# Second block's two modulated norms: latent and context parts signalled apart, all latent chunks first at the second norm, three preparing operations moved

## Reference

```
for layer in range(2):
    u  = rms_norm_2(h,  norm_g[layer]) * (1 + scale)   + shift
    uc = rms_norm_2(hc, norm_g[layer]) * (1 + scale_c) + shift_c
    layer 0: y, yc = ab_mixer(u, uc, ...)     # in projections of u and uc, two attentions
    layer 1: y, _  = c_mixer(u, uc, ...)      # q, k, v, z = split(u @ in_w); q_c, k_c, v_c, z_c of uc
    h = h + gate * y;   hc = hc + gate_c * yc # context only in layer 0
return rms_norm_2(h, final_g)
```

## Time and profile before

| | us |
|---|---|
| median of three runs | 2233.18 |
| the profiled execution | 2232.56 |
| its span | 2230.2 |
| PE busy | 2177.5 |
| DVE busy | 1262.2 |
| ACT busy | 903.3 |

### The profile page before, as it was taken

How to read it: one execution, slowest core, us unless ns; L and a number is a source line. 1 busy time by engine, 2 the same in 40 slices (tenths; PEclk the granted TensorE clock), 3 DMA queues, 4 the chain that set the end, 5 groups by cost and what they waited for, 6 DMA issues and landing times.

```text
span 2230.2 us, 31483 instructions
## 1 busy us (share of the span) xinstructions
PE 2177.5 (98%) x12755; PEld 1784.1 (80%) x12755; DVE 1262.2 (57%) x1752; ACT 903.3 (41%) x1575; POOL 289.0 (13%) x215
## 2 busy tenths in 40 slices
PE   7999999999999999999999999999999999999998
PEld 6776688778888776688778888989888887888777
DVE  4687548984224687548983226422666636212794
ACT  4447843222214447843222223232565524212673
POOL 2001322121222001322121000000010000000230
PEclk9999999999999999999999999999999999999999
DMA  5220016543563220025543322132000122321221
GB/s 164 90 71 2 1 61 204 183 145 80 149 171 91 90 71 1 1 67 198 189 146 79 135 95 60 48 101 72 15 23 9 52 76 94 123 68 57 72 72 57
DMA packets 149106, 194.26 MB, mean 87 GB/s; under 512 B 43165, under 2 KB 96426, under 8 KB 148962
## 3 DMA queue, kind: packets, MB, share of 16 engines
q1 hardware_dynamic: 110288, 169.83, 23.4%
q10 hardware_dynamic: 38514, 22.26, 3.8%
q0 software_dynamic: 160, 0.16, 0.0%
HBM read 180.51 MB, written 11.72 MB: 86 GB/s over the span
## 4 chain that ended last, share of the span: by engine, by line
PE 89%; DVE 5%; ACT 3%; issue 2%; DMA 0%; ACTq 0%; POOLq 0%; DVEq 0%
PE ps L536 69%; PE ps L2779 3%; PE ps L1903 3%; PE ps L2796 2%; PE ps L2808 2%; PE ps L2317 1%; PE ps L2274 1%; PE ps L2303 1%; DVE probs_t L2118 1%; PE ps L2784 1%; PE ps L1937 1%; ACT probs_t L2885 1%; DVE neg_max L2085 1%; PE ps L2782 1%; PE ps L744 1%
## 5 line engine op out<-in xcount | busy, mean ns | idle before, releaser
L501 DVE TENSOR_TENSOR w_low<-w_raw,w_high 128x2048 fp32r<-128x2048 f32 (+4 forms) x140 | 303.1, 2165 | 493.1 <-ACT w_high L496 493.0
L496 ACT ACTIVATE w_high<-w_raw 128x2048 fp32r<-128x2048 f32 (+4 forms) x140 | 253.2, 1808 | 574.0 <-PE ps L536 550.6
L536 PE MATMUL ps<-h_hi,w_high 128*128 128x512 f32 (+1 forms) x1168 | 439.7, 376 | 3.0 <-DVE w_low L501 2.2
L536 PE MATMUL ps<-h_lo,w_high 128*128 128x512 f32 (+1 forms) x1168 | 437.1, 374 | 0.0
L536 PE MATMUL ps<-h_hi,w_low 128*128 128x512 f32 (+1 forms) x1168 | 436.8, 374 | 0.0
L536 PEld LDWEIGHTS ps<-h_hi,w_high 128*128 128x128 f32 x1168 | 219.9, 188 | 53.9 <-issue 10.5
L536 PEld LDWEIGHTS ps<-h_hi,w_low 128*128 128x128 f32 x1168 | 219.8, 188 | 39.8
L536 PEld LDWEIGHTS ps<-h_lo,w_high 128*128 128x128 f32 x1168 | 220.0, 188 | 39.0 <-issue 0.5
L536 PE MATMUL ps<-w_high,h_hi 128*128 128x512 f32 (+3 forms) x576 | 215.0, 373 | 0.7 <-DVE h_lo L3181 0.7
L536 PE MATMUL ps<-w_low,h_hi 128*128 128x512 f32 (+3 forms) x576 | 212.1, 368 | 0.0
L536 PE MATMUL ps<-w_high,h_lo 128*128 128x512 f32 (+3 forms) x576 | 211.8, 368 | 0.0
(11 more groups left out here) (395 smaller groups left out, 3674.3 us busy)
## 6 DMA issues: line engine op xcount, KB each, us to landing
w_raw<-in_w_gate_up SPq DMA_DIRECT2D x44, 1024.0 KB, 5.1
ada_w<-in_ada_w SPq DMA_DIRECT2D x24, 1024.0 KB, 5.2
w_raw<-in_w_down SPq DMA_DIRECT2D x20, 1024.0 KB, 5.0
w_raw<-in_w_in SPq DMA_DIRECT2D x16, 1024.0 KB, 5.1
w_raw<-in_c_in_w SPq DMA_DIRECT2D x16, 1024.0 KB, 5.8
w_raw<-in_w_out SPq DMA_DIRECT2D x8, 1024.0 KB, 4.8
w_raw<-in_ab_in_w SPq DMA_DIRECT2D x8, 1024.0 KB, 5.2
masked_scratch<-mask_table ACTq DMA_DIRECT2D x8, 512.0 KB, 3.6
```

The costliest lines, as they stand in the source:

```text
L496: e.activation(w_high[j % 2][:, 0:size], w_raw[j % 2][:, 0:size], ACT.Copy).then_inc(sig.w_high_done, 1)
L501: e.tensor_tensor(w_low[j % 2][:, 0:size], w_raw[j % 2][:, 0:size], w_high[j % 2][:, 0:size].bitcast(F32), ALU.subtract).then_inc(sig.w_lo ...
L536: mm = e.matmul(dst, lhs, rhs, start=start and a == 0, stop=stop and a == 2)
```

## The change

`full_ready`, `part_high` and `part_low` now count latent parts alone, and `ctx_full`, `ctx_high` and `ctx_low` count the context's. At the first norm (`l == 0`) the parts alternate, latent and context of chunk 0, of chunk 1 and so on, and `full` runs one part ahead of `low`. At the second norm all eight latent chunks come first, `full` and `low` of a chunk right behind each other, then the eight context parts, paired. `ModGain`'s operations move from ahead of the reciprocal to behind the second staging copy of the first norm. The product behind the first norm waits for a context chunk at tile 4; the product that first reads the context of layer 1 waits for all of it once. The load of `gate_first` also waits for the second norm's transposes, which are long done when it is issued.

```diff
+                            if self.context_paced and i == 0 and n == NT:
+                                e.wait_ge(sig.ctx_low, B["ctx_low"] - self.paced + k + 1)
+                            if self.context_whole and i == 0 and n == 0 and k == 0:
+                                e.wait_ge(sig.ctx_low, B["ctx_low"])
...
+                self.l, self.sum_bank, self.wide_banks, self.context, self.gains = l, sum_bank, wide_banks, context, gains
+                self.full, self.high, self.low = (sig.full_ready, sig.ctx_full), (sig.part_high, sig.ctx_high), (sig.part_low, sig.ctx_low)
+                self.full_name, self.high_name, self.low_name = ("full_ready", "ctx_full"), ("part_high", "ctx_high"), ("part_low", "ctx_low")
+                self.parts = [(k, v) for k in range(KD) for v in range(2)] if l == 0 else [(k, v) for v in range(2) for k in range(KD)]
...
-                for k in range(KD):
-                    e.wait_ge(sig.full_ready, B["full_ready"] + k + 1)
-                    for src, nt, t0, v in self.halves:
-                        ins = e.activation(h2_hi[:, k, t0:t0 + nt], mod_full[:, k % 2, t0:t0 + nt], ACT.Identity, bias=self.shift(k, v))
-                    ins.then_inc(sig.part_high, 1)
-                    if k == 4:
+                for k, v in self.parts:
+                    _, nt, t0, _ = self.halves[v]
+                    e.wait_ge(self.full[v], B[self.full_name[v]] + k + 1)
+                    e.activation(h2_hi[:, k, t0:t0 + nt], mod_full[:, k % 2, t0:t0 + nt], ACT.Identity, bias=self.shift(k, v)).then_inc(self.high[v], 1)
+                    if (k, v) == (4, 1 - self.l):
...
+                if self.gains:
+                    self.gains.make(e, B, ch)
+                    e.wait_ge(sig.mod_ready, B["mod_ready"] + 1)
...
+                def full(k, v):
+                    src, nt, t0, _ = self.halves[v]
                     if k >= 2:
-                        e.wait_ge(sig.part_low, B["part_low"] + k - 1)
...
+                        e.wait_ge(self.low[v], B[self.low_name[v]] + k - 1)
...
-                def low(k):
-                    e.wait_ge(sig.part_high, B["part_high"] + k + 1)
-                    for src, nt, t0, v in self.halves:
-                        ins = e.scalar_tensor_tensor(out=h2_lo[:, k, t0:t0 + nt], in0=mod_full[:, k % 2, t0:t0 + nt], scalar=self.shift(k, v),
-                                                     in1=h2_hi[:, k, t0:t0 + nt].bitcast(F32), op0=ALU.add, op1=ALU.subtract)
-                    ins.then_inc(sig.part_low, 1)
-                    if k == 4:
+                    if k == 0:
+                        e.wait_ge(sig.inverse_wide, B["inverse_wide"] + v + 1)
+                    dst, x, inv = mod_full[:, k % 2, t0:t0 + nt], src[:, k, :], ps[:, self.wide_banks[v], 0:nt]
+                    if self.l and v == 0:
+                        cuts = [(by_blocks(dst)[:, :, j], by_rows(x)[:, :, j], by_rows(inv)[:, :, j]) for j in range(4)]
+                    else:
+                        cuts = [(dst, x, inv)]
+                    for dst, x, inv in cuts:
+                        ins = e.scalar_tensor_tensor(out=dst, in0=x, scalar=self.gain(k, v), in1=inv, op0=ALU.mult, op1=ALU.mult)
+                    ins.then_inc(self.full[v], 1)
+
+                def low(k, v):
+                    _, nt, t0, _ = self.halves[v]
+                    e.wait_ge(self.high[v], B[self.high_name[v]] + k + 1)
+                    e.scalar_tensor_tensor(out=h2_lo[:, k, t0:t0 + nt], in0=mod_full[:, k % 2, t0:t0 + nt], scalar=self.shift(k, v),
+                                           in1=h2_hi[:, k, t0:t0 + nt].bitcast(F32), op0=ALU.add, op1=ALU.subtract).then_inc(self.low[v], 1)
+                    if (k, v) == (4, 1 - self.l):
                         cut_low(e, B, 1, 2048)
...
-                full(0)
-                low(0)
-                full(1)
-                for k in range(1, KD):
-                    if k + 1 < KD:
-                        full(k + 1)
-                    low(k)
+                if self.l:
+                    for k, v in self.parts[:KD]:
+                        full(k, v)
+                        low(k, v)
+                    paired = self.parts[KD:]
+                else:
+                    paired = self.parts
+                full(*paired[0])
+                for now, after in zip(paired, paired[1:]):
+                    full(*after)
+                    low(*now)
+                low(*paired[-1])
...
+            def make(self, e, B, ch):
                 e.wait_ge(sig.mod_landed, B["mod_landed"])
...
+                e.wait_ge(sig.inverse_wide, B["inverse_wide"])
...
-        mod_norms = [ModNorm(0, 6, (7, 0), context), ModNorm(1, 0, (1, 2))]
+        mod_norms = [ModNorm(0, 6, (7, 0), context, ModGain()), ModNorm(1, 0, (1, 2))]
...
-            context, ModGain(),
+            context,
...
+                b.context_paced = a.l == 0
...
+            if isinstance(b, PairAhead):
+                a.context_whole = True
```

More of the change, by code:

```diff
@@ L383, in build_program @@
         sig.full_ready = semaphore("full_ready")
+        sig.ctx_full = semaphore("ctx_full")
+        sig.ctx_high = semaphore("ctx_high")
+        sig.ctx_low = semaphore("ctx_low")
         sig.part_high = semaphore("part_high")
@@ L548, in build_program @@
             paced = 0
+            context_paced = context_whole = False
             chase = False
@@ L3079, in build_program, with __init__ @@
             chase = True
-            late = ("part_high", "part_low", "full_ready", "sq_ready", "sq_added")
-            def __init__(self, l, sum_bank, wide_banks, context=None):
-                self.l, self.sum_bank, self.wide_banks, self.context = l, sum_bank, wide_banks, context
+            late = ("part_high", "part_low", "full_ready", "ctx_high", "ctx_low", "ctx_full", "sq_ready", "sq_added")
+            def __init__(self, l, sum_bank, wide_banks, context=None, gains=None):
+                self.l, self.sum_bank, self.wide_banks, self.context, self.gains = l, sum_bank, wide_banks, context, gains
+                self.full, self.high, self.low = (sig.full_ready, sig.ctx_full), (sig.part_high, sig.ctx_high), (sig.part_low, sig.ctx_low)
+                self.full_name, self.high_name, self.low_name = ("full_ready", "ctx_full"), ("part_high", "ctx_high"), ("part_low", "ctx_low")
+                self.parts = [(k, v) for k in range(KD) for v in range(2)] if l == 0 else [(k, v) for v in range(2) for k in range(KD)]
                 self.halves = [(x_t, S, 0, 0), (xc_t, CTX, S, 1)]
@@ L3087, in __init__ @@
                 self.counts = {"sq_ready": self.nv * KD, "sq_added": self.nv * (KD - 1), "sum_step": 1, "root_ready": 1, "inv_ready": 1,
-                               "staged_ready": 2, "inverse_wide": 2, "full_ready": KD, "part_high": KD, "part_low": KD}
+                               "staged_ready": 2, "inverse_wide": 2, "full_ready": KD, "part_high": KD, "part_low": KD,
+                               "ctx_full": KD, "ctx_high": KD, "ctx_low": KD}
+                if gains:
+                    self.counts.update(gains.counts)
             def gain(self, k, v):
@@ L3151, in tensor @@
                     mm.then_inc(sig.inverse_wide, 1)
-                    release(bank, B, ("full_ready", KD))
+                    release(bank, B, (self.full_name[v], KD))
             def vector(self, e, B, L, ch):
@@ L3159, in vector @@
                     e.tensor_copy(mod_stage[:, a:b, :], bc(mod_inv[:, a:b].unsqueeze(2), [P, b - a, P])).then_inc(sig.staged_ready, 1)
-                def full(k):
+                if self.gains:
[3 more added lines that the diff above has]
+                    src, nt, t0, _ = self.halves[v]
                     if k >= 2:
-                        e.wait_ge(sig.part_low, B["part_low"] + k - 1)
-                    if k == 4 and self.context:
+                        e.wait_ge(self.low[v], B[self.low_name[v]] + k - 1)
+                    if (k, v) == (4, 1) and self.context:
@@ L3176, in full @@
-                    ins.then_inc(sig.full_ready, 1)
-                def low(k):
-                    e.wait_ge(sig.part_high, B["part_high"] + k + 1)
-                    for src, nt, t0, v in self.halves:
-                        ins = e.scalar_tensor_tensor(out=h2_lo[:, k, t0:t0 + nt], in0=mod_full[:, k % 2, t0:t0 + nt], scalar=self.shift(k, v),
-                                                     in1=h2_hi[:, k, t0:t0 + nt].bitcast(F32), op0=ALU.add, op1=ALU.subtract)
-                    ins.then_inc(sig.part_low, 1)
-                    if k == 4:
-                        cut_low(e, B, 1, 2048)
```

7 lines of the change are left out of this document (2 added, 5 removed).

## The result

The changed kernel takes 2238.83 us, median of nine runs (2237.0 to 2243.75), against 2232.79 for nine runs of the kernel before (2230.14 to 2235.79): 6.0 us slower, ratio 1.0028, interval 1.0020 to 1.0037. The prediction said 2239.3.

What follows compares the result with a forecast made beforehand. PE bounds the kernel, busy 2177.5 of 2230.2 us. Profiled 2232.56 us with -0.9 (first norm), +5.7 (piece 3) and +1.6 (clock), together +6.4, gives 2239.0; stated as 2239.3 for the median, range 2236.2 to 2241.4.

Steps and rivals of the forecast that it cites:

- The held cut: Second norm, ACT's queue: context parts stand ahead of the cut of piece 2, so group 1 starts 6.3 us later.
- The standstill: Gate product, ahead of group 1: PE waits for piece 2 from 1876.3 to 1884.1, 7.8 us.
- the period of 0.91 us: Second norm's context block on DVE: one `full` starts 0.91 us after another, 0.78 if semaphore waits cost nothing.
- The clock: Behind PE's idle time ahead of group 1: one stretch at 1.2 GHz costs 1.6 us, bounds 0 to 3.3.
- The rival of a full clock: Group 1: PE's clock stays full, or an existing low stretch falls away; 2237.8 us, chance 0.17.
- Piece 3: Gate product, group 1's second half: old wait gone, start at 1895.0 instead of 1889.24, +5.7 us.
- Piece 1: Gate product, chunk 4 at the second norm: PE starts at 1865.24 instead of 1866.76, -1.5 us.
- `h_lo`'s wait: Second norm, chunk 1: PE's 0.8 us wait lies ahead of a later wait and pays nothing of its own.
- First norm: Product behind the first norm starts at 1369.0 instead of 1369.91, the filler now ending the wait: -0.9 us.
- Nothing gave it back: After the gate product: later work does not recover the delay; opposite case 2235.6 us, chance 0.07.

Runs made afterwards that it cites:

- Alternating: Changed kernel with latent and context parts alternating at the second norm too, instead of latents first; 2230.27 us, ratio 0.9991 to the kernel before.
- unpaired parts: Changed kernel with the second norm's context parts one by one, `low` right behind its `full`; 2241.17 us in one run.
- three buffers: Changed kernel with three instead of two buffers for the context's `full` at the second norm; 2235.67 us in one run.
- filler kernel: Changed kernel with 36 more filler matmuls between groups 0 and 1 of the gate product; 2237.22 us, ratio 1.0022 to the kernel before.
- all cuts ahead: Changed kernel with parts alternating at both norms and the gate product's pieces 1, 2 and 3 cut earlier; 2227.39 us, ratio 0.9975 to the kernel before.

## Why the prediction was right

- **The held cut** was the step on which everything hung. The standstill was forecast at 7.8 us and is 7.74; the period of 0.91 us was read from two rows of before and came out to the hundredth. Alternating removes it, unpaired parts add 4.0 us, three buffers take 0.75 off.
- **The clock**: right in kind, not in size. +1.6 was forecast for one stretch at 1.2 GHz. Group 1's first half took 12.95 us, and 10.88 is what its matmuls took at full clock in the earlier trace rows, so 2.07 were lost on the matmuls; but most of this does not arrive, as PE would have had to wait for piece 3. The filler kernel, whose clock stays full, gains 0.86 us. The rival of a full clock is out for every profile in which the standstill was left empty; of the other runs only their mean granted clock is known, 0.996 on average over the changed kernel's nine runs and 0.998 over the filler kernel's.
- **Piece 3**: its wait is gone, but not for the reason given; this is the step that was wrong. The prediction took ACT's way from the table load to the cut from before, 8.94 us, and found a margin of 0.2 us. It took 9.83 (1885.09 to 1894.92), as ACT waited for stores of `zc_out` twice, 1.43 and 3.79 us, and not once for 3.88. The piece was ready at 1896.87 + 2.29 = 1899.16, 11.7 us behind group 1's start, and at full clock PE asks for it after 10.88: in the changed kernel it comes without a wait only because the low clock delays the request to 1900.40. The filler kernel shows the wait (0.91). The two terms, piece 3 and clock, were -0.6 + 1.6 = +1.0 and came out at +1.51 together.
- **Piece 1** comes 1.46 us earlier from the norm's first `full` (-1.5). On PE's own line only 1.25 arrive (-0.13 and -1.12), since that first `full` starts 0.2 later in this execution, whose seven filler matmuls ahead of the transposes took 1.52 us where they took 1.32 before. That `h_lo`'s wait would pay nothing of its own is borne out: it is gone, and the gain is that of the cut.
- **First norm**: -0.9 forecast, -1.28 measured. Two sizes were too small, both because the end of a matmul in the view overlaps the next one's start. The seven filler matmuls read as 1.47 us, but the transposes start 1.30 behind them, so the transposes come 0.38 earlier and the filler of 14 comes 0.44 earlier, not 0.25; and the product starts 2.50 behind that filler's start, not 2.67.
- **The sum and its luck**: 2232.56 + 6.4 and the 0.6 up to the median make 2239.6; the forecast of 2239.3 lies 0.3 below its own sum, with no reason given. The first norm's gain was 0.4 too small and the loss at piece 3 and the clock 0.5 too small, and they nearly cancel. So that the median is met to 0.5 us, with single runs from 2237.0 to 2243.75, is in part luck; that the kernel would be some 6 us slower, and where, is not.
- **Nothing gave it back**: behind 1900 the two executions differ by 0.16 us over 341.

## What to carry to other kernels

Work that has slack of its own is not free to be put into one block: look at what is queued behind the block on each in-order engine, and when the engine that sets the time will ask for it. Where an engine already idles inside a loop waiting for another (here 0.79 us in each chunk), the slack work belongs in that hole. Price a delay at the place where the waiting engine picks up again. What its clock loses there counts only as far as no later wait would have taken up the same time: here 2.07 us were lost on matmuls, and filling the standstill gave back 0.86.

## What the runs showed of the hardware

- DVE starts a 256-column operation 0.39 us behind its predecessor when it waits for nothing, and 0.51 to 0.52 behind when it waits for that one's semaphore, though either lasts 0.48 (1871.29 to 1871.68 in the kernel with three buffers; 1877.17 to 1877.69 in the changed one). The Trainium skill ("VectorE: DVE Perf Modes", "The DRAIN you can't avoid") reports a semaphore behind each of eight copies as costing nothing extra. Here the measurement decides: sixteen operations with six such waits were 0.75 us longer.
- TensorE's clock went to 1.2 GHz and back in stretches that some executions have and others don't, in code that is the same: around 934 and 1547 us in the changed kernel's profile (granted 0.50 and 0.63), in neither of those of before and of the alternating kernel, both again in the filler kernel's (0.57 in 932 to 940, 0.72 in 1545 to 1551), and the second in that of all cuts ahead (0.57 in 1544 to 1548). In the changed kernel the two stand beside a shift of 2.73 us ahead of the first norm and of 1.56 between the norms, more than most parts of this change are worth.
- A low clock just ahead of a standstill costs nothing: in the kernels with three buffers and with unpaired context group 0 ran partly at 1.2 GHz, and group 1 still started where DVE's queue alone put it (34.56 and 39.33 us). The standstill was shorter by the same amount.
